# Group 1's first feed-forward in pairs of seven half products, with arrays kept in DRAM over it and selection of group 0 in 20 loops

## What is computed

```python
x <- LN1(alpha*x + 0.5*SwiGLU_1(x))
x <- LN2(alpha*x + W_mix_out[conv_group(x) | dsa_group(x)])
x <- LN3(alpha*x + MemCrossAttn(x, mem))
x <- LN4(alpha*x + 0.5*SwiGLU_2(x))

def _swiglu(x, w_gate, w_up, w_down):
    return (jax.nn.silu(x @ w_gate) * (x @ w_up)) @ w_down

score = jnp.where(admissible[None], score, -jnp.inf)   # in _dsa_attention
_, idx = lax.top_k(score, top_k)
```

## Time and profile before

| | us |
|---|---|
| median of 3 runs (2514.77 to 2514.97) | 2514.92 |
| the profiled execution | 2520.49 |
| span of the profiled execution, first to last instruction | 2518.70 |

### The profile page before, as it was taken

One profiled execution on the slowest core, in us unless ns is written; L12 is line 12 of the kernel. 1 busy time (PEld: TensorE's weight loads), 2 busy tenths in 40 slices (PEclk: granted clock), 3 DMA queues, 4 the chain that ended last, 5 costly groups with the idle time before them and its releaser, 6 DMA issues.

```text
span 2518.7 us, 40246 instructions
## 1 busy us (share of the span) xinstructions
PE 2427.3 (96%) x16095; PEld 2202.2 (87%) x16095; DVE 1081.7 (43%) x1999; ACT 1030.3 (41%) x1877; POOL 1337.6 (53%) x860
## 2 busy tenths in 40 slices
PE   8999999999999999998999999999989999999997
PEld 8888889888999999987689987888659898899997
DVE  1000002265810004277452598998163435565443
ACT  4333332543333233445544533323373535545341
POOL 4776665544666666423162676766503426556563
PEclk9999999999999999999899999999999999999999
DMA  4444532453233232432121233333402212343332
GB/s 144 123 121 117 159 94 73 140 150 103 83 94 92 84 88 77 137 111 93 67 79 51 68 94 99 110 99 94 159 25 75 60 43 76 106 137 94 114 88 69
DMA packets 425664, 245.01 MB, mean 97 GB/s; under 512 B 23008, under 2 KB 415328, under 8 KB 424720
## 3 DMA queue, kind: packets, MB, share of 16 engines
q1 hardware_dynamic: 389712, 197.88, 27.4%
q10 hardware_dynamic: 33200, 32.56, 4.0%
q0 software_dynamic: 2576, 12.07, 1.3%
HBM read 218.79 MB, written 21.74 MB: 96 GB/s over the span
## 4 chain that ended last, share of the span: by engine, by line
PE 82%; DVE 5%; ACT 5%; POOL 3%; issue 2%; DMA 2%; ACTq 0%; DVEq 0%; POOLq 0%
PE LIN L1016 68%; PE LIN L936 7%; PE TR L1360 1%; POOL WL L2543 1%; PE LIN L1093 1%; PE TR L1069 1%; ACT WH L1412 1%; POOL XL L2626 1%; PE LIN L1308 1%; ACT PR L1946 1%; ACT PT L1971 1%; PE TR L1347 1%; PE TR L1170 1%; DVE SC L2154 1%; DVE PR L2482 1%
## 5 line engine op out<-in xcount | busy, mean ns | idle before, releaser
L2543 POOL TENSOR_TENSOR WL<-WRAW,WH 128x1024 fp32r<-128x1024 f32 (+1 forms) x342 | 802.3, 2349 | 450.0 <-ACT WH L1412 445.0
L1016 PE MATMUL LIN<-XH,WH 128*128 128x256 f32 (+3 forms) x2456 | 722.0, 325 | 20.1 <-DVE Y L2222 6.5
L1016 PE MATMUL LIN<-XH,WL 128*128 128x256 f32 (+3 forms) x2456 | 715.0, 322 | 0.0
L1016 PE MATMUL LIN<-XL,WH 128*128 128x256 f32 (+3 forms) x2456 | 714.7, 322 | 0.0
L1016 PEld LDWEIGHTS LIN<-XH,WH 128*128 128x128 f32 (+1 forms) x2456 | 440.0, 190 | 60.7 <-issue 21.9
L1016 PEld LDWEIGHTS LIN<-XL,WH 128*128 128x128 f32 (+1 forms) x2456 | 439.6, 190 | 34.0
L1016 PEld LDWEIGHTS LIN<-XH,WL 128*128 128x128 f32 (+1 forms) x2456 | 438.2, 189 | 33.8
L1016 PE MATMUL LIN<-HH,WH 128*128 128x256 f32 (+2 forms) x1632 | 464.9, 307 | 1.5 <-POOL HL L2667 1.1
L1016 PE MATMUL LIN<-HL,WH 128*128 128x256 f32 (+2 forms) x1632 | 462.1, 305 | 0.0
L1016 PE MATMUL LIN<-HH,WL 128*128 128x256 f32 (+2 forms) x1632 | 461.4, 305 | 0.0
L1412 ACT ACTIVATE WH<-WRAW 128x1024 fp32r<-128x1024 f32 (+2 forms) x346 | 355.7, 1029 | 135.6 <-DMA WRAW<-in_ffn_down 33.0
(11 more groups left out here) (247 smaller groups left out, 3188.2 us busy)
## 6 DMA issues: line engine op xcount, KB each, us to landing
WRAW<-in_ffn_gate SPq DMA_DIRECT2D x79, 512.0 KB, 3.8
WRAW<-in_ffn_up SPq DMA_DIRECT2D x79, 512.0 KB, 3.8
WRAW<-in_ffn_down SPq DMA_DIRECT2D x64, 512.0 KB, 3.7
WRAW<-in_w_mix_in SPq DMA_DIRECT2D x44, 512.0 KB, 3.9
WRAW<-in_ffn_down SPq DMA_DIRECT2D x32, 384.0 KB, 3.3
WRAW<-in_w_mix_out SPq DMA_DIRECT2D x16, 512.0 KB, 3.6
WRAW<-in_w_mem_q SPq DMA_DIRECT2D x16, 512.0 KB, 3.7
WRAW<-in_w_mem_o SPq DMA_DIRECT2D x16, 512.0 KB, 3.7
```

What stands on the lines that cost most here:

```text
L1016: last = pe.matmul(LIN[0:pr.rows, pr.slot, out:out + w], wt[:, SLOT[pr.tile], c, 0:pr.rows], x[:, c, col:col + w], start=(c == 0 and wt is ...
L2543: pool.tensor_tensor(WL[:, SLOT[n], 0:nk, 0:width], raw(n)[:, 0:nk, 0:width], WH[:, SLOT[n], 0:nk, 0:width].bitcast(F32), ALU.subtract).th ...
```

## The change

FOLDED also holds (1, 1), the first feed-forward of group 1, again with 4, 8 and 6 pairs.

- `fold_strands` hangs the sums of activations on the middle and end of product 4 (two each) and their low parts on the ends of products 4 to 7, now for both folded feed-forwards. In the first, the sums are made from Y, which holds alpha times x, so high and low part carry a factor 1/alpha.
- What lies in the room of TF, TH and TL is kept: at the end of group 1's load segment ScalarE issues seven stores (`kept`) of KPA, KPB, KSA, VP and VS (128 x 512 each) and MKT and MV (128 x 2048 each), ahead of the last two spills; the strand `("restore",)`, behind the last pair, issues seven loads back. VectorE waits for the stores ahead of the sums, later readers and writers of the arrays for the loads (`keep_moved`).
- Selection of group 0 is cut into 20 loops, strands `("select some", n, ...)`, with 32 rounds in all: 2 at the end of each of products 0 to 3; 1, 2, 2, 1 at the first four down products of part 0; 2, 3, 3, 2 at those of part 1; 2, 2, 1, 1, 1, 1 at the six products behind the last pair; the cut at the last.
- WRAWX has a second place, at `r_ahead`, for the pairs of the first feed-forward; SP waits for the transposes of token tile 4 ahead of its first load there.

```diff
-FOLDED = [(2, 1)]
+FOLDED = [(1, 1), (2, 1)]
...
+def fold_strands(ffn, g, which):
+
+    ffn[RING].mid.append(("fold sums", which, 0))
+    ffn[RING].end.append(("fold sums", which, 1))
+    for k in range(4):
+        ffn[RING + k].end.append(("fold part", which, k))
...
+        if folded(1, g):
+            fold_strands(ffn, g, 1)
+            run = [k for k, pr in enumerate(ffn) if isinstance(pr, Pair)]
+            ffn[run[-1] + 1].mid.append(("restore",))
         if g.index == 1:
-            ffn[2 * RING].mid.append(("select", 0))
+            downs = [[pr for pr in ffn if pr.kind == "down" and pr.part == part] for part in range(2)]
+            tail = ffn[run[-1] + 1:run[-1] + 7]
+            rounds = [(pr, 2) for pr in ffn[0:4]] + list(zip(downs[0][0:4], (1, 2, 2, 1)))
+            rounds += list(zip(downs[1][0:4], (2, 3, 3, 2))) + list(zip(tail, (2, 2, 1, 1, 1, 1)))
...
+            for pr, n in rounds:
+                left -= n
+                pr.end.append(("select some", n, left == 0))
...
+        held = [KPA[:, 0:HALF], KPB[:, 0:HALF], KSA[:, 0:PAST], VP[:, 0:4, :].rearrange("p k q -> p (k q)"),
+                VS[:, 0:4, :].rearrange("p k q -> p (k q)"), MKT[:, :, :].rearrange("p k q -> p (k q)"),
+                MV[:, :, :].rearrange("p k q -> p (k q)")]
...
+                    if IN_PAIR[n].which == 1:
+                        sp.wait_ge(back_done, LOAD_AT[1] + len(GROUPS[1].tiles))
...
+                    act.activation(TH[:, k, :, 0:w], TF[:, k, :, 0:w], ACT.Copy, scale=1.0 / ALPHA if which == 1 else 1.0)\
+                        .then_inc(fold_hi, 1)
+                elif kind == "restore":
+                    act.wait_ge(part_done, 7 * [two for two in PLAN.pairs if two.which == 1][-1].q + 7)
+                    for there, here in zip(kept, held):
+                        act.dma_start(here, there[:, :]).then_inc(keep_moved, 16)
...
+                    all_moved()
+                    act.wait_ge(tok_read, len(GROUPS[0].tiles))
+                    for there, here in zip(kept, held):
+                        act.dma_start(there[:, :], here).then_inc(keep_moved, 16)
                     spill_conv(GROUPS[0], KC - 1)
...
+                if which == 1:
+                    dve.wait_ge(residual, MEM_AT + len(g.tiles))
+                    dve.wait_ge(keep_moved, HELD)
...
+            def select_some(g, n, ends):
+                tiles = score_tiles(g)
+                keys_of = [SC[0:rows, SCORE_AT[(g.index, t)]:SCORE_AT[(g.index, t)] + keys] for t, rows, keys, _ in tiles]
+                with dve.Fori(0, n):
+                    for i, sc in enumerate(keys_of):
+                        dve.max(M8[0:tiles[i][1], i, :], sc)
+                    dve.drain()
+                    for i, sc in enumerate(keys_of):
+                        dve.match_replace(sc, M8[0:tiles[i][1], i, :], sc, TAKEN)
+                    dve.drain()
```

More of the change, by code:

```diff
@@ L384, in back @@
         if folded(2, g):
-            ffn[RING].mid.append(("fold sums",))
-            for k in range(4):
-                ffn[RING + k].end.append(("fold part", k))
+            fold_strands(ffn, g, 2)
             for k in range(KD // 2):
@@ L678, in encoder_step @@
         TR = ctx.enter_context(nc.psum_tensor("TR", [P, 2, 1024], F32))
+        kept = [nc.dram_tensor(f"kept{i}", [P, a.shape[1]], F32, kind="Internal").ap() for i, a in enumerate(held)]
+        HELD = 16 * len(held)
         spill_q = [nc.dram_tensor(f"spill_q{i}", [P, KC, GC], F32, kind="Internal").ap() for i in range(2)]
@@ L895, in _ @@
                     sp.wait_ge(lo_split, COUNT[before])
-                if RAW_AT[n] >= 2 and (n < 4 or n - 4 not in IN_PAIR):
-                    sp.wait_ge(product, [pr for pr in PLAN.products if pr.name == "memo"][-1].p + 1)
+                if RAW_AT[n] >= 2 and (RAW_BEFORE[n] is None or stage_of(IN_PAIR[RAW_BEFORE[n]]) != stage_of(IN_PAIR[n])):
+                    if IN_PAIR[n].which == 1:
+                        sp.wait_ge(back_done, LOAD_AT[1] + len(GROUPS[1].tiles))
+                    else:
+                        sp.wait_ge(product, [pr for pr in PLAN.products if pr.name == "memo"][-1].p + 1)
                 sp.dma_start(raw(n)[:, 0:nk, 0:width], weight[name][:, row:row + nk, c0:c0 + width])\
@@ L1603, in tokens @@
                 act.wait_ge(tok_done, k + 1)
+                if g.sample:
+                    act.wait_ge(keep_moved, 2 * HELD)
                 if k >= 2:
@@ L2110, in fold, with fold_tokens @@
                         sum_low(following, i)
-            def fold_tokens():
+            def fold_tokens(which, second):
                 g = current[0]
[L2114 to L2117, removed]
+                w, k0 = g.cols // 2, 4 * FOLDED.index((which, g.index))
+                if which == 1:
+                    dve.wait_ge(residual, MEM_AT + len(g.tiles))
+                    dve.wait_ge(keep_moved, HELD)
+                else:
+                    for h in range(2):
+                        dve.wait_ge(x_hi[h], KD * (3 + 2 * g.index + 1))
                 b11, b12 = Y[:, 0:4, 0:w], Y[:, 0:4, w:2 * w]
@@ L2179, in select @@
                     last.then_inc(selected, 1)
+            def select_some(g, n, ends):
[8 more added lines that the diff above has]
+                    dve.drain()
+                if ends:
+                    for sc in keys_of:
+                        dve.tensor_scalar(sc, sc, CUT, FAR, ALU.is_gt, ALU.mult)
             def last_norm(k, t, rows, buf, stored):
@@ L2362, in take_up @@
                 elif kind == "fold sums":
-                    fold_tokens()
+                    fold_tokens(*what)
                 elif kind == "fold part":
                     fold_low(*what)
+                elif kind == "select some":
+                    select_some(GROUPS[0], *what)
                 elif kind == "select":
```

36 lines of the change are left out of this document (23 added, 13 removed).

## The result

The changed kernel took **2523.07 us** (median of 8 runs), the kernel before 2514.94 on the same chips: a ratio of 1.0027, with a 95% interval of 1.0018 to 1.0037. It is slower by 0.3%, 8.1 us. The forecast was 2512.8 with a range of 2508 to 2522, so it had the wrong sign and its range missed the time by 1 us.

A forecast was written before the change was run, and what follows sets the result against it. TensorE, busy 96% of the span, was taken to bound the kernel. Pairs -22.4, entry +19.8 and later selection +0.5 gave -2.1 us, so 2514.92 became 2512.8 us, range 2508 to 2522.

The forecast's parts named there:

- What each pair saves: Group 1's first feed-forward: a folded pair takes 10.65 us against 11.97 plain, saving 1.32; 17 pairs gain 22.4 us.
- dear pairs: Rival, chance 0.07: all pairs run at 11.46 us, as in part 0 of the second feed-forward; time 2526.5.
- The entry: Start of group 1: stores and selection rounds put the first pair's end at 655.4; costs 19.8 us, from 16.4 to 27.4.
- up to 5.1: VectorE's four sums and four low parts contending with GpSimd for SBUF: up to 5.1 us more, most already counted.
- R: When ScalarE's wait for the spills ends, before HH's first write in group 1: 608.8 us, dear bound 613.9.
- Selection later: Rounds in down stages hidden by VectorE's idle time; tail ready 25.2 us after the last pair, wanted at 26.8; 0.5 allowed.
- dear loops: Rival, chance 0.13: 20 short selection loops at 1.5 us each, 9.2 us together at entry and tail; time 2522.
- Restoring: Seven loads behind the last pair, 3.41 MB, about 11 us: costs nothing, or 2 us if a weight tile arrives late.
- Sum: Whole kernel: -22.4 + 19.8 + 0.5 = -2.1 us of span, so 2514.92 becomes 2512.8 us.

The follow-up runs named there:

- e4: Changed kernel with restoring loads spread over the down stage, stores spread over group 0's mixing and entry rounds moved to down products; 2494.81 us, 0.9916 of before.
- e7: Changed kernel with the two spills at the entry issued ahead of the seven stores, the same nine issues; 2520.79 us.
- e5: Changed kernel with the eight entry selection rounds moved behind the first seven down products of parts 0 and 1, everything computed; 2506.63 us.
- e1: Changed kernel with the seven restoring loads issued one by one behind down products 0, 2, 4, ... of part 2; 2515.19 us.
- e3: Changed kernel with the seven stores issued one by one behind seven products of group 0's mixing, not at the entry; 2516.53 us.
- e6: Changed kernel with only the two 1024 KB restoring loads moved behind two down products of part 2, five of 256 KB staying; 2514.68 us.

## Why the prediction was wrong, by its own steps

- **What each pair saves: right.** From the first pair's end to the last one's the changed kernel took 922.92 - 657.2 = 265.7 us, where the earlier trace rows gives 923.75 - 635.6 = 288.1: 22.4 less, as summed. Part 0 runs at 10.6, so "dear pairs" falls. That the 11.46 of the earlier trace rows came from scaling Y fits, since nothing scales Y here, but no run took the scaling away by itself.
- **The entry: right in form, 2.5 us too small.** The first pair ends at 657.2 (652.78 and the 4.46 that the last pair takes from there to its evacuation), 64.2 us after the start against 41.9 plain: 22.3, where I had 19.8 and a range of 16.4 to 27.4. Half of the 2.5 is ahead of the first sum (36.9 us after the start where the forecast has 35.7), half behind it (27.3 where I took 26.0). Of the second half the clock has its part: the third half product came 17.9 us after the first sum, but the last five took 9.3 us instead of 7.6, at a granted clock of 0.51 in the row of 648 to 650. VectorE's sums and low parts of activations took 1.28 to 1.29 us each but for two low parts of 1.89 and 1.38, 0.7 us over in all, where the prediction's estimate was up to 5.1. The slow cases do stand behind GpSimd: the 1.89 began 0.24 us behind GpSimd's FP of 636.10, and in e4 one sum took 2.40, begun 0.04 us behind a GpSimd instruction of 1.30.
- **R, the wait for the spills: the number right, its weight wrong.** HH came at 610.24, close behind my 608.8. But taking the wait away (e7) is worth 0.3 us (0.2 to 0.8 by the idle times of the three traces with this entry), since VectorE's queue is as late: it starts on a low part of tile 2 that I took from before, ended at 602.9, and that ended at 605.8 here because ScalarE's issues held its copy. From there VectorE's queue alone gives the 630. I had costed the spills' bytes and never ScalarE's own time: at the entry an issue is 0.35 us in the earlier trace rows, and here they grew to as much as 1.65, nine in 7.6 us. Only without the rounds does the wait for the spills set the entry, as e5 shows (6.28 us). The terms that I printed behind R add up to 20.4, not 20.6, and put tile 4's low part at R + 8.4, not 9.0; in the trace it came at 618.32, 8.1 behind HH. That moves nothing else.
- **Selection later: right.** The loops showed gaps of 0.3 to 0.4 us, the cut started at 944.27, took 2.13 and was wanted at 957.75. My 0.5 us and "dear loops" (9.2) both fall.
- **Restoring: this is the step that failed.** "Weight tiles share the engines but have a ring of four tiles ahead: nothing, or 2 us if one arrives over 8 us late." The tile did arrive some 7 us late, and it cost 7.9 us. Two things were wrong in the sentence, the ring and what is late behind a late tile. The ring of four is that of WH and WL; the raw tile goes into one of two buffers, and the folded form frees the last of them late. Before, the first down tile was issued 8.4 us ahead of ScalarE's copy of it, as SP's and ScalarE's rows of the kernel before show (the issue stands merged with five more; the second copy behind it is its own, the first being that of the up tile):

```profile
921.90 31.77 SPq L899 DMA_DIRECT2D WRAW<-in_ffn_down  x6
...
930.32 1.05 ACT L1412 ACTIVATE WH<-WRAW 128x1024 fp32r<-128x1024 f32 x1
```

  Now it is issued at 930.98, and ScalarE is free for it at 931.3. And a tile that is late for ScalarE is late for everything behind it there: TensorE did not lack weights, it lacked the evacuation of a finished product (<-ACT FG L1512). I had asked who reads the tile, and not what is queued behind its first reader.
- **Sum.** Forecast: -22.4 + 19.8 + 0.5 = -2.1. In the trace: -22.4 + 22.3 + 7.9 = +7.8, against 8.1 measured. The tail is three quarters of the miss (7.4 of 9.9).

The slower side did hold, though by none of its rivals' mechanisms: no rival had a cost in the tail other than the loops'.

## What to carry to other kernels

When a transfer off the path is placed, look at the few us behind its issue for the next tile that is issued just in time, and at what stands behind that tile's reader on an engine that works in order; count ring slots at the buffer that the DMA writes. Here the bulk DMAs that nobody wanted soon were free when they stood one by one in a long stretch of steady work (e1, e3), and dear in a bunch at a change of stage. A DMA issue is also work of the engine that issues it: nine in a row took 7.6 us here, where one takes 0.35.

## What the runs showed of the hardware

- **DMA issues in a row on ScalarE's queue took longer, unevenly.** At the entry the stores and spills took 0.35 us for the first, 1.65 for MKT's and 0.50 for MV's behind it; in e5, 0.35 rising to 1.78 for spill_ch. In the tail seven loads of the same sizes took 0.33 to 0.46 each, 3.2 us in all. Whether the direction or the token tiles' loads and spills ahead in the queue make the difference was not tried.
- **A weight tile behind other loads landed last.** 0.52 MB issued last behind 3.41 MB took 10.2 us to be usable; alone it takes 3.6 (e1), behind 1.31 MB 4.7 (e6). By the page's DMA table the last of the seven loads (MV) landed 9.9 us after its issue at 929.81, so the tile came just behind it. The two queues did move nearly packet for packet from 935 to 938 (156 and 121), but the bytes stood 1.16 to 0.06 MB.
- **No one rate fits every stretch.** The Trainium skill (DMA: Bandwidth & Descriptors, Specifications) gives about 358 GB/s as HBM's limit for one core. The row of 936 to 941 has just this mean, but it is no limit here: the two microseconds from 936 to 938, loads alone, moved 426 GB/s, and 602 to 607 at the entry, stores and a weight tile, 433. So the 401 GB/s of the earlier trace rows, a stretch of stores, was no bad choice for R.
- **Half clock after TensorE's idle.** The granted clock was 0.50 after the 5.16 us wait at 942.88 (row of 943 to 944). In the same work it was 1.00 after a wait of 2.04 in e6 (944 to 946) and after 0.69 in e1. At the entry it was 0.50 from 619 to 624, behind the wait of 8.22.
